# Block 3 of the last convolution made on GpSimd instead of TensorE

## The reference

```python
def _conv_mixer(h, w_in, dw, db, ln_g, ln_b, w_out):
    a, b, g = jnp.split(h @ w_in, 3, axis=-1)
    y = a * jax.nn.sigmoid(b)
    y = lax.conv_general_dilated(y, dw[:, None, :], window_strides=(1,),
        padding=[(15, 15)], dimension_numbers=('NWC', 'WIO', 'NWC'),
        feature_group_count=BRANCH) + db
    y = jax.nn.silu(_layernorm(y, ln_g, ln_b)) * jax.nn.silu(g)
    return y @ w_out
```

## Time and profile before

| | us |
|---|---|
| median of 3 runs (1143.63 to 1144.26) | 1143.94 |
| the profiled execution | 1143.82 |
| its span | 1142.0 |
| busy in the span: TensorE / VectorE / GpSimd / ScalarE | 909.9 / 769.5 / 318.9 / 339.0 |

### The profile page before, as it was taken

One profiled execution on the slowest core, in us unless ns is written; L12 is line 12 of the kernel. 1 busy time (PEld: TensorE's weight loads), 2 busy tenths in 40 slices (PEclk: granted clock), 3 DMA queues, 4 the chain that ended last, 5 costly groups with the idle time before them and its releaser, 6 DMA issues. The chain is left out here.

```text
span 1142.0 us, 20885 instructions
## 1 busy us (share of the span) xinstructions
PE 909.9 (80%) x8392; PEld 703.9 (62%) x8392; DVE 769.5 (67%) x2042; ACT 339.0 (30%) x820; POOL 318.9 (28%) x285
## 2 busy tenths in 40 slices
PE   8999999887687696686424356898878667999998
PEld 8998688765565484465202124786555333788887
DVE  4765646787898865865468878788787666943411
ACT  2511101235322222312011122677575022253100
POOL 0001000234344343433334444434545430000000
PEclk9999999989898697898655567899999659999999
DMA  8998695999999999999999999999999995473201
GB/s 333 419 376 323 257 416 225 401 421 422 387 424 421 419 422 423 421 422 421 426 418 421 414 420 420 420 401 420 420 409 421 421 421 215 167 295 111 74 1 38
DMA packets 51856, 402.70 MB, mean 353 GB/s; under 512 B 5808, under 2 KB 8240, under 8 KB 9392
## 3 DMA queue, kind: packets, MB, share of 16 engines
q0 software_dynamic: 40320, 293.62, 62.5%
q1 hardware_dynamic: 10432, 105.70, 22.8%
q10 hardware_dynamic: 1008, 2.06, 0.5%
HBM read 400.31 MB, written 1.05 MB: 351 GB/s over the span
## 5 line engine op out<-in xcount | busy, mean ns | idle before, releaser
L498 POOL DMA_INDIRECT arena<-uv_dram,arena x194 | 231.6, 1194 | 333.8 <-PE ps L737 267.2
L1860 DVE CUSTOM_DVE_ANT_0 arena<-arena 128x1024 f32<-128x1024 f32 x194 | 235.0, 1224 | 83.7 <-DMA arena<-uv_dram,arena 80.8
L737 PE MATMUL ps<-arena 128*32 128x256 f32 x1552 | 134.0, 475 | 159.9 <-DVE arena L1896 159.7
L737 PEld LDWEIGHTS ps<-arena 128*32 128x32 f32 x1552 | 47.2, 127 | 226.0 <-DVE arena L1896 193.6
L1304 ACT ACTIVATE gel<-dots 128x2 f32<-128x2 f32 x128 | 26.0, 203 | 387.2 <-DVE dots L1860 365.6
L552 PEld LDWEIGHTS ps<-xn,wring 128*128 128x128 f32 x896 | 109.6, 203 | 9.8 <-issue 6.9
L552 PE MATMUL ps<-xn,wring 128*128 128x128 f32 x896 | 112.7, 288 | 2.6 <-DMA wring<-units_dram 2.6
L1860 DVE CUSTOM_DVE_ANT_0 wring<-wring,arena 128x1024 f32<-128x1024 f32 x62 | 75.3, 1224 | 46.0 <-DMA wring<-uv_dram,arena 45.3
L498 POOL DMA_INDIRECT wring<-uv_dram,arena x62 | 74.0, 1193 | 114.6 <-PE ps L737 105.2
L737 PE MATMUL ps<-wring,arena 128*32 128x256 f32 x496 | 42.7, 473 | 53.2 <-DVE arena L1896 53.1
L1896 DVE TENSOR_SCALAR arena<-const,gel,arena 128x32 f32<-128x32 f32 x256 | 65.3, 307 | 28.3 <-ACT gel L1304 22.0
(11 more groups left out here) (336 smaller groups left out, 1478.6 us busy)
## 6 DMA issues: line engine op xcount, KB each, us to landing
wring<-units_dram SPq DMA_DIRECT2D x39, 2048.0 KB, 12.0
arena<-mod_dram POOLq DMA_DIRECT2D x24, 1024.0 KB, 7.2
arena<-units_dram SPq DMA_DIRECT2D x8, 2048.0 KB, 10.5
arena<-uv_dram,arena POOLq DMA_INDIRECT x194, 14.4
wring<-units_dram SPq DMA_DIRECT2D x2, 1024.0 KB, 8.6
hA<-x_t_dram SPq DMA_DIRECT2D x2, 512.0 KB, 7.6
arena<-mem_t_dram SPq DMA_DIRECT2D x1, 1024.0 KB, 10.7
arena<-keys_dram ACTq DMA_DIRECT2D x2, 512.0 KB, 6.8
```

What stands on the lines that cost most here:

```text
L498: pool.indirect_dma_start(row(n), None, uv_d, bass.IndirectOffsetOnAxis(ap=idx[:, n:n + 1], axis=0)).then_inc(sem(f"row_in{b}"), 16)
L737: mm = pe.matmul(acc_ps(q)[G * c:G * (c + 1), :], lhsT=diag[:, s % 2, j, :], rhs=row(n)[:, D + 256 * c:D + 256 * (c + 1)], start=(p == 0 a ...
L1860: post(V.tensor_tensor_reduce(out=row(n)[:, 0:D], in0=row(n)[:, 0:D], in1=x_rep[q % 2], scale=1.0, scalar=0.0, op0=ALU.mult, op1=ALU.add, ...
```

## The change

Block 3 (`POOL_BLOCK`) leaves TensorE's list and goes to GpSimd's, behind its last indirect DMA. GpSimd does each tap in two instructions: a product of 143 columns by the tap into one of two tiles (`pool_odd`), and a sum into `yc`; the first tap is one instruction with the bias. Four blocks (`FIRST_QUAD` = 4 to 7) stay on TensorE, and the tiles that go with block 3 disappear: one of five `first_copies`, a fifth of the columns of each `last_copies`, one of VectorE's five weight tiles. `mean_sums` takes block 3 behind TensorE's four, before VectorE's three. The memset of `idle` goes from GpSimd to VectorE's start, and two semaphores are merged into one (`tap_operands`).

```diff
-            pool.memset(idle, 0.0).then_inc(sem("idle_zero"), 1)
...
+            need(pool, "glu", KB + 8)
+            out = yc[:, POOL_BLOCK, CUT:S]
+            for tap in range(CV_TAPS):
+                w = col("cv_dw", 8 * tap + POOL_BLOCK)
+                x = ypad[:, POOL_BLOCK, CUT + tap:S + tap]
+                if tap == 0:
+                    last = post(pool.tensor_scalar(out, x, w, col("cv_db", POOL_BLOCK), ALU.mult, ALU.add), "pool_tap")
+                else:
+                    post(pool.tensor_scalar(pool_odd[tap % 2], x, w, None, ALU.mult), "pool_tap")
+                    need(pool, "pool_tap", 2 * tap)
+                    last = post(pool.tensor_tensor(out, out, pool_odd[tap % 2], ALU.add), "pool_tap" if tap < CV_TAPS - 1 else "conv_pool")
...
-                need(pe, "y4", KB - DVE_BLOCKS + 4)
+                need(pe, "tap_operands", KB * CHUNKS + KB - FIRST_QUAD + 4)
...
-                order = list(range(DVE_BLOCKS, KB)) + list(range(DVE_BLOCKS))
+                order = list(range(FIRST_QUAD, KB)) + [POOL_BLOCK] + list(range(DVE_BLOCKS))
...
+                    elif k == POOL_BLOCK:
+                        need(pe, "conv_pool", 1)
...
-            last_half("cv_g0", 1, xn, later={(0, 0): lambda: conv_blocks(3, 4), (1, 0): lambda: conv_blocks(5, 6)})
+            last_half("cv_g0", 1, xn, later={(0, 0): lambda: conv_blocks(4), (1, 0): lambda: conv_blocks(5, 6)})
...
+                    go(V.memset(idle, 0.0), "pads")
...
-            for b in range(DVE_BLOCKS, KB):
+            for b in range(FIRST_QUAD, KB):
```

More of the change, by code:

```diff
@@ L115 @@
 TILES += [f"cv{b}" for b in range(KB)]
-TILES += [f"y4a{b}" for b in range(3, KB)] + [f"y4b{g}" for g in range(4)] + [f"conv{b}" for b in range(3, KB)] + ["mean", "var", "ss_m1.0", "ss_m1.1"]
+TILES += [f"y4a{b}" for b in range(4, KB)] + [f"y4b{g}" for g in range(4)] + [f"conv{b}" for b in range(4, KB)] + ["mean", "var", "ss_m1.0", "ss_m1.1"]
 TILE_NO = {n: i for i, n in enumerate(TILES)}
@@ L167 @@
 DVE_BLOCKS = 3
+POOL_BLOCK = DVE_BLOCKS
+FIRST_QUAD = POOL_BLOCK + 1
 Y4_COLS = S - CUT + 4 * (QUADS - 1)
@@ L214, in build @@
         gel = sb("gel", [P, 2, BATCH])
-        arena = sb("arena", [P, 34308 + 20 * Y4_COLS])
+        arena = sb("arena", [P, 34308 + 16 * Y4_COLS])
         ps = ctx.enter_context(nc.psum_tensor("ps", [P, 8, 512], F32))
@@ L331, in build @@
         gT, ycn = (blocks(area(4096 + 2048 * i, 2048), KB) for i in range(2))
-        quads = {b: area(a, 1024) for b, a in zip(range(DVE_BLOCKS, KB), (8192, 9216, 10240, 11264, M3 + 3056))}
-        y4 = area(34308, 20 * Y4_COLS).rearrange("p (b g x) -> p b g x", b=KB - DVE_BLOCKS, g=4)
+        quads = {b: area(a, 1024) for b, a in zip(range(FIRST_QUAD, KB), (8192, 9216, 10240, 11264))}
+        y4 = area(34308, 16 * Y4_COLS).rearrange("p (b g x) -> p b g x", b=KB - FIRST_QUAD, g=4)
+        pool_odd = [area(M3 + 3056 + (S - CUT) * i, S - CUT) for i in range(2)]
         sq_all = blocks(area(8192, 2048), KB)
@@ L684, in conv_chunk @@
                 b, taps = chunk_taps(c)
-                need(pe, "tap_diag", c + 1)
+                need(pe, "tap_operands", c + 1)
                 if c % CHUNKS == 0:
@@ L713, in last_copies @@
                 n = Y4_COLS - Y4_FIRST
-                post(shifted_copies(f"y4b{g}", g, lambda i: ypad[:, DVE_BLOCKS:, CUT + i + Y4_FIRST:CUT + i + Y4_COLS], slice(0, (KB - DVE_BLOCKS) * n)),
+                post(shifted_copies(f"y4b{g}", g, lambda i: ypad[:, FIRST_QUAD:, CUT + i + Y4_FIRST:CUT + i + Y4_COLS], slice(0, (KB - FIRST_QUAD) * n)),
                      "tiles")
             def conv_quads(b):
-                need(pe, "tap", b - DVE_BLOCKS + 1)
+                need(pe, "tap", b - FIRST_QUAD + 1)
                 out = tile_begin(f"conv{b}")
@@ L723, in conv_quads @@
                         mm = pe.matmul(out[G * g:G * (g + 1), 0:S - CUT], lhsT=quads[b][:, (4 * i + g) * G:(4 * i + g + 1) * G],
-                                       rhs=y4[:, b - DVE_BLOCKS, g, 4 * i:4 * i + S - CUT], start=(i == 0), stop=(i == QUADS - 1))
+                                       rhs=y4[:, b - FIRST_QUAD, g, 4 * i:4 * i + S - CUT], start=(i == 0), stop=(i == QUADS - 1))
                 post(mm, "tiles")
@@ L756, in slot @@
                         token_transposes(g)
-                if 0 <= s - Y4_SLOT < KB - DVE_BLOCKS:
-                    first_copies(DVE_BLOCKS + s - Y4_SLOT)
+                if 0 <= s - Y4_SLOT < KB - FIRST_QUAD:
+                    first_copies(FIRST_QUAD + s - Y4_SLOT)
             def chain(t, step):
@@ L995, in products_of @@
                     pe.matmul(ps[:, 3, S:S + P], lhsT=tile, rhs=tile, start=True, stop=True)
-            need(pe, "idle_zero", 1)
+            need(pe, "pads", 1)
             products_of(idle, 22)
@@ L1259, in diagonals @@
                     ins = act.activation(tap_chunk[c % 3][:, i], ident, ACT.Copy, scale=col("cv_dw", 8 * tap + b))
-                post(ins, "tap_diag")
+                post(ins, "tap_operands")
             def conv_out(b):
@@ L1293, in slot @@
                         gate_tokens(g)
-                if 0 <= s - Y4_SLOT - 1 < KB - DVE_BLOCKS:
+                if 0 <= s - Y4_SLOT - 1 < KB - FIRST_QUAD:
                     i = s - Y4_SLOT - 1
-                    name = f"y4a{DVE_BLOCKS + i}"
+                    name = f"y4a{FIRST_QUAD + i}"
                     tile_ready(act, name)
                     tile_used_wait(act, act.copy(y4[:, i, :, 0:Y4_FIRST], blocks(tile_ps(name)[:, 0:4 * Y4_FIRST], 4)), name)
-                    signal(act, "y4")
+                    signal(act, "tap_operands")
                 act.wait_ge(sem("dots"), BATCH * (s + 1))
@@ L1590, in _ @@
                 tile_ready(act, f"y4b{g}")
-                n = (KB - DVE_BLOCKS) * (Y4_COLS - Y4_FIRST)
-                tile_used_wait(act, act.copy(y4[:, :, g, Y4_FIRST:], blocks(tile_ps(f"y4b{g}")[:, 0:n], KB - DVE_BLOCKS)), f"y4b{g}")
-                signal(act, "y4")
+                n = (KB - FIRST_QUAD) * (Y4_COLS - Y4_FIRST)
+                tile_used_wait(act, act.copy(y4[:, :, g, Y4_FIRST:], blocks(tile_ps(f"y4b{g}")[:, 0:n], KB - FIRST_QUAD)), f"y4b{g}")
+                signal(act, "tap_operands")
             gate_silu("cv_g0", 0)
-            for b in range(DVE_BLOCKS, KB):
+            for b in range(FIRST_QUAD, KB):
                 tile_ready(act, f"conv{b}")
@@ L2298, in _ @@
                 dve.wait_ge(sem(f"row_free{b}"), GATHERS // RING)
-            for b in range(DVE_BLOCKS, KB):
-                w = cols[:, COLS["cv_quads"][0] + 32 * (b - DVE_BLOCKS):COLS["cv_quads"][0] + 32 * (b - DVE_BLOCKS + 1)]
+            for b in range(FIRST_QUAD, KB):
+                w = cols[:, COLS["cv_quads"][0] + 32 * (b - FIRST_QUAD):COLS["cv_quads"][0] + 32 * (b - FIRST_QUAD + 1)]
                 post(V.tensor_tensor(blocks(quads[b], 32), cst("stack").unsqueeze(1).broadcast_to([P, 32, G]),
@@ L2482 @@
     taps = np.concatenate([a["cv_dw_2"][0], np.zeros((4 * QUADS - CV_TAPS, D), f4)])
-    parts_ready = {"cv_quads": taps.reshape(QUADS, 4, KB, 4, G)[:, :, DVE_BLOCKS:].transpose(1, 4, 2, 0, 3).reshape(P, -1)}
+    parts_ready = {"cv_quads": taps.reshape(QUADS, 4, KB, 4, G)[:, :, FIRST_QUAD:].transpose(1, 4, 2, 0, 3).reshape(P, -1)}
     cols = np.concatenate([colmajor(parts[n]) if n in parts else parts_ready[n] if n in parts_ready else
```

6 lines of the change are left out of this document (3 added, 3 removed).

## The result

The changed kernel takes 1154.5 us (median of 4 runs, 1153.65 to 1155.25), the kernel before, beside it on the same chip, 1143.8: ratio 1.0095, 95% interval 1.0083 to 1.0107.

A forecast was written before the change was run, and what follows sets the result against it. TensorE bounds the kernel, VectorE close behind. GpSimd would end at 1025.5 and the mean at 1028.6 instead of 1004.6, 24.0 us later, the 2.8 saved being spent waiting: 1143.8 + 24.0 = 1167.8, so 1168 us, range 1155 to 1184.

The forecast's parts named there:

- What TensorE saves: Before the mean: one convolution block gone, 2.08 us, and four narrower copies, 0.7 us; together 2.8 us.
- Code load hidden, edits at nothing: GpSimd's code load fits the some 35 us from 935 us; weight tile, first copy, memset and merged semaphore cost nothing.
- A tap's price: GpSimd's block: product 0.33, sum 0.44, two waits 0.10, together 0.87 us a tap, costed from its memsets.
- The low end of the price: GpSimd's tap at 0.44 us, passes overlapped: GpSimd ends at 1013.4 and the time is 1156 us.
- the forecast's own theory: VectorE's trains keep GpSimd out; 28 taps remain once VectorE ends at about 1001.1 us; chance 0.70.
- So GpSimd gets in at the start and at the two seams between blocks: Beside VectorE's three trains GpSimd fits only some 3 of 31 taps until 999.6 us; the other 28 follow.
- Half clock: TensorE, after waiting some 25 us, runs at 1.2 GHz for 2.6 us, costing 1.3 us.
- GpSimd's end: GpSimd's last tap: 28 taps at 0.87 us, 24.4 us after about 1001.1, done at 1025.5 us.
- the way from there to the mean's end: On TensorE: 0.05 us wait, 1.8 us of the mean's products, 1.3 us of lowered clock; mean ends at 1028.6.
- turns: Rival: VectorE and GpSimd alternate by instruction, GpSimd's time lengthening VectorE's trains; 1158 to 1164 us, chance 0.15.
- Side by side: Rival: neither engine holds up the other, GpSimd ends at 999.0 and the time is 1141.0 us; chance 0.06.

The follow-up runs named there:

- the pause of 1.94 us: Changed kernel, with GpSimd's sixth tap made to wait for VectorE's 21st multiply-add of its first block: 1158.3 us.
- the probes: Changed kernel with all four blocks on VectorE and single GpSimd instructions on unrelated tiles begun inside VectorE's trains, two runs: 1151.9 and 1151.5 us.

## Why the prediction was wrong

The direction, the place and the kind of wait were right: TensorE gets to the mean's fifth product early, waits there for GpSimd, and comes out at half clock. The steps one by one:

- *What TensorE saves:* forecast 2.8 us, measured 2.56 from VectorE's copy to the mean. The copies went from 0.88 to 0.75 us, not by a fifth of their time.
- *Code load hidden, edits at nothing:* no row speaks against it. GpSimd's first product began at 972.90, 0.18 behind the copy.
- *A tap's price:* 0.87 us forecast, 1.18 measured alone. The memsets were too cheap a neighbour: the product by a column's scalar took 0.65, twice the 0.33 forecast, while the sum's 0.46 was near the 0.44, and the one pause of 0.08 near the 0.10 taken for waits. (The low end of the price, 0.44 us, had no waits in it; with them the time that it gave would have been some 3 us higher.) With this price and the forecast's own theory GpSimd would have ended 8.7 us later still (28 x 0.31).
- *"So GpSimd gets in at the start and at the two seams between blocks [...] some 3 taps of 31 until 999.6 us"*: **the step that failed.** 22 taps were done by 1000 us. The earlier trace rows are real, and the fresh products in the last trains of the probes waited in the same way; but they show an instruction that arrives late in an undisturbed train. The changed kernel's stream begins with the train, 0.02 us before its first multiply-add, and comes back within 0.1 us each time; the pause of 1.94 us that shut it out shows that it has to come back in time, or the train closes. I had carried a rule from single instructions over to a stream.
- *Half clock:* 1.3 us forecast, 2.3 measured.

GpSimd's end came 14.8 us earlier than forecast (1010.7 for 1025.5) and the way from there to the mean's end 0.7 later (3.8 for 3.1): that is the 14.1 by which the mean's end was missed (1014.5 for 1028.6). Two errors of opposite sign met in the first figure: 8.7 us for the tap, and some 23.5 for the shutting out. That the time came within 0.5 us of the range is luck.

Of the rivals, *turns* named what happened in the trace, evenly spaced sums and wider gaps in VectorE's trains, but its time (1158 to 1164) let VectorE lose all or most of GpSimd's instructions: 0.56 to 0.77 us a tap where it was 0.38. *Side by side* said that a tap of 1.2 us would give 1150; with a tap of 1.23 and the 2.3 us of half clock that is close to the time measured, since for GpSimd, unlike for VectorE, the two engines do stand nearly side by side.

The Trainium skill, "SBUF — State Buffer", section "Who interferes with whom", says that a VectorE instruction with two SBUF inputs contends with a GpSimd instruction that reads SBUF, and one with a single SBUF input, outside its two-port modes, does not. The runs agree: with the sums in PSUM a train takes 0.277 us a multiply-add beside GpSimd as without it. The section "SBUF: two separate sides" of the same page of the Trainium skill says that the first to begin holds the pair of ports for its whole instruction and the other fully blocks. There they differ: VectorE lost 0.11 us to a product of 0.70, and a product begun 1.57 us into a train waited for 24 multiply-adds, not for one. By these measurements a late arrival waits for the train and not for one instruction of it.

What stays open is why a train closes after four to six multiply-adds: the runs don't tell a number of instructions from a time, or from how far VectorE has read ahead.

## What to carry to other kernels

A wait seen between two engines holds for the pattern of arrival that it was seen in: before a stalled single instruction is made a rule, ask whether the new work comes singly or as a stream, and when it begins. If GpSimd is to help VectorE, the first question is how many SBUF tiles VectorE's instruction reads, the second what GpSimd's instructions cost on a tile of this very size and form; here a running sum in PSUM, a broadcast tap in place of a scalar and a product one ahead turned +10.7 us into -2.2. An engine that helps another at 0.38 us of its time for each tap may help by less than nothing: four blocks on VectorE alone were done 2.4 us sooner than three with GpSimd's fourth beside them.

## What the runs showed of the hardware

- GpSimd's product of 143 fp32 columns took 0.65 us with the scalar taken from a column, 0.42 us as a product of two tiles, one of them broadcast: the form that reads one tile was the slower one.
- A wait for GpSimd's own last result left a pause of 0.083 us, and without it instructions overlapped by some 0.04 us.
- A GpSimd product that came late in a VectorE train waited up to 7.10 us, until 0.5 us behind the train's end; a stream of GpSimd begun with the train lost 0.06 us a tap, and VectorE 0.38.
